# Modulation vectors, X's norm product and the first projection of a three-block transformer kernel: last quarters on TensorE, the product on ScalarE, three jobs begun by halves

## The reference, cut to what matters

```python
mod = c @ w_ada + b_ada            # c: 1024 values, w_ada: 1024 x 3072
shift, scale, gate = split(mod, 3)
xn = x * rsqrt(mean(x * x) + eps)
h = xn * g_norm * (1 + scale) + shift
proj = h @ w_in                    # 1024 x 5120, ten jobs of 512 columns
```

## Time and profile before

| | us |
|---|---|
| median of 3 runs (2044.94 to 2055.8) | 2050.69 |
| the profiled execution | 2051.03 |
| its span, first to last instruction | 2049.2 |
| TensorE busy | 1952.9 |
| VectorE busy | 1529.3 |
| ScalarE busy | 1262.1 |
| first matmul of the first projection starts | 30.62 |
| its second halves start | 51.22 |

### The profile page before, as it was taken

The page is one execution under the profiler, slowest core; times in us unless marked ns, Lnnn a source line. Parts: engine busy times, 40 slices in busy tenths (PEclk is TensorE's granted clock), DMA queues, the critical chain, the costliest instruction groups (busy, mean ns, idle before and its releaser), DMA issues. The chain is left out here.

```text
span 2049.2 us, 25968 instructions
## 1 busy us (share of the span) xinstructions
PE 1952.9 (95%) x9557; PEld 1611.3 (79%) x9557; DVE 1529.3 (75%) x1725; ACT 1262.1 (62%) x1366; POOL 95.1 (5%) x99
## 2 busy tenths in 40 slices
PE   4999998999999899999999999999999999999997
PEld 3887776788887788888888888888888878778876
DVE  7656766554577688889898888989988874467675
ACT  3544564534355477778777787877778764546453
POOL 0000300000000320000000000000000000000000
PEclk9999999999999999999999999999999999999999
DMA  9763644555552399999999999999999985524400
GB/s 354 250 226 131 206 154 164 176 187 185 164 185 83 117 391 371 380 381 368 385 364 379 377 378 377 364 394 365 371 387 365 386 298 180 190 79 154 144 1 31
DMA packets 186125, 535.14 MB, mean 261 GB/s; under 512 B 12465, under 2 KB 23749, under 8 KB 186054
## 3 DMA queue, kind: packets, MB, share of 16 engines
q1 hardware_dynamic: 179808, 518.95, 69.4%
q10 hardware_dynamic: 4422, 8.92, 1.2%
q0 software_dynamic: 1824, 6.31, 1.1%
HBM read 521.02 MB, written 13.12 MB: 261 GB/s over the span
## 5 line engine op out<-in xcount | busy, mean ns | idle before, releaser
L1107 DVE TENSOR_TENSOR WL<-ring,WH 128x2048 fp32r<-128x2048 f32 x475 | 1073.6, 2281 | 282.9 <-ACT WH L1103 279.6
L1103 ACT ACTIVATE WH<-ring 128x2048 fp32r<-128x2048 f32 x475 | 902.0, 1912 | 383.6 <-PE bank L457 352.2
L455 PE MATMUL bank<-WH,XTH 128*128 128x512 f32 (+3 forms) x1904 | 751.1, 394 | 19.1 <-DVE XTL L1852 6.5
L457 PE MATMUL bank<-WH,XTL 128*128 128x512 f32 (+3 forms) x1904 | 740.0, 389 | 0.0
L456 PE MATMUL bank<-WL,XTH 128*128 128x512 f32 (+3 forms) x1904 | 739.6, 388 | 0.0
L455 PEld LDWEIGHTS bank<-WH,XTH 128*128 128x128 f32 x1904 | 361.9, 190 | 105.3 <-DVE WL L1107 26.3
L457 PEld LDWEIGHTS bank<-WH,XTL 128*128 128x128 f32 x1904 | 361.7, 190 | 74.4
L456 PEld LDWEIGHTS bank<-WL,XTH 128*128 128x128 f32 x1904 | 362.2, 190 | 69.6 <-issue 0.2
L455 PE MATMUL bank<-WH,HTH 128*128 128x512 f32 (+1 forms) x568 | 219.9, 387 | 3.2 <-DVE HTL L2037 1.5
L457 PE MATMUL bank<-WH,HTL 128*128 128x512 f32 (+1 forms) x568 | 217.8, 383 | 0.0
L456 PE MATMUL bank<-WL,HTH 128*128 128x512 f32 (+1 forms) x568 | 217.7, 383 | 0.0
(11 more groups left out here) (420 smaller groups left out, 1358.2 us busy)
## 6 DMA issues: line engine op xcount, KB each, us to landing
ring<-in_od_we_gate SPq DMA_DIRECT2D x112, 1024.0 KB, 7.1
ring<-in_od_we_up SPq DMA_DIRECT2D x112, 1024.0 KB, 8.1
ring<-in_od_we_down SPq DMA_DIRECT2D x112, 1024.0 KB, 8.2
ring<-in_w_in SPq DMA_DIRECT2D x20, 1024.0 KB, 5.7
ring<-in_fox_w_in SPq DMA_DIRECT2D x16, 1024.0 KB, 6.3
ring<-in_nsa_w_in SPq DMA_DIRECT2D x14, 1024.0 KB, 5.1
ring<-in_w_ada SPq DMA_DIRECT2D x12, 1024.0 KB, 10.0
ring<-in_ev_w_in SPq DMA_DIRECT2D x12, 1024.0 KB, 5.2
```

Of the source, the lines that this page charges most:

```text
L455: nc.tensor.matmul(out, x[0], wt[0][:, k, :], start=start, stop=False, skip_group_check=check)
L457: return nc.tensor.matmul(out, x[1], wt[0][:, k, :], start=False, stop=stop, skip_group_check=check)
L1103: nc.scalar.activation(wh, slot_ap(n, nk, width), ACT.Copy).then_inc(hi_made, 1)
L1107: nc.vector.tensor_tensor(wl, slot_ap(n, nk, width), wh.bitcast(F32), ALU.subtract).then_inc(lo_made, 1)
```

## The change

```diff
+        def ada_part(kind, h, part):
+            n = chunk(kcols(w["w_ada"], {"scale": D, "shift": 0}[kind] + 512 * h, 512, 4 * part, 4), 4, 512)
+            ada[n] = kind, h, 4 * part, 4
+            if part and kind == "shift":
+                direct[n] = h
...
+            def out(self, c, tt):
+                return bank[4 + tt if c == 2 and self.by_parts == 3 else (2 * c + tt) % 4]
...
-                    if part == 0 and c >= 2:
+                    if part == 0 and c >= max(2, by_parts):
                         pe.wait_ge(proj_act, self.ba + c - 1)
...
+                        if (c, part, tt) in beside and k == 0:
+                            beside[c, part, tt]()
...
+                elif n in direct:
+                    eng.sem_inc(lo_made, 1)
                 elif n in ada:
...
                     reach(sp, lo_made, n - RING + 1, n)
+                if n - RING in direct:
+                    sp.wait_ge(ada_cols, 3 * direct[n - RING] + 2)
...
+            rms_act(act, XN)
+            scaled(act, "act_root")
+            for tt in range(TT):
+                nc.scalar.activation(XN[:, tt, :], X[:, tt, :], ACT.Copy, scale=stat[:, tt:tt + 1]).then_inc(xn_set, 1)
+            split_until(act, c_in1[0][0][0] + 1)
             act.dma_start(small[:, :], t["small"][0:NSM].partition_broadcast(128)).then_inc(small_in, 16)
             act.dma_start(co[:, :], t["co"]).then_inc(small_in, 16)
...
-            rms_act(act, XN)
-            split_until(act, c_in1[0][0][0] + 1)
...
             x_columns(1)
-            split_until(act, c_in1[0][1][0] + 1)
+            split_until(act, c_in1[2][0][0] + 1)
             act.wait_ge(ada_set, 4)
...
             rms(dve)
-            scaled(dve)
-            for tt in range(TT):
-                nc.vector.tensor_scalar(XN[:, tt, :], X[:, tt, :], stat[:, tt:tt + 1], None, ALU.mult).then_inc(xn_set, 1)
+            split_until(dve, 2)
...
             for h in range(2):
-                split_until(dve, c_in1[0][h][0])
-                out = bank[4 * h]
-                dve.wait_ge(ada_cols, 2 * h + 1)
+                if h:
+                    split_until(dve, c_in1[2][0][0] + 1)
+                dve.wait_ge(ada_cols, 3 * h + 1)
...
-                dve.wait_ge(ada_cols, 2 * h + 2)
-                nc.vector.tensor_tensor(SHIFT[:, 4 * h:4 * h + 4], bank[4 * h + 1][:, 0:4], vec_rows("b_ada", 4 * h, 4),
-                                        ALU.add).then_inc(ada_set, 1)
+                split_until(dve, c_in1[0][0][0] + 1 if h == 0 else c_in1[0][1][0])
+                dve.wait_ge(ada_cols, 3 * h + 3)
+                link(dve, nc.vector.tensor_tensor(shift_h, bank[4 * h + 1][:, 0:4], vec_rows("b_ada", 4 * h, 4), ALU.add))
+                nc.vector.tensor_tensor(shift_h, shift_h, bank[4 * h + 1][:, 4:8], ALU.add).then_inc(ada_set, 1)
                 dve.wait_ge(ada_set, 2 + 2 * h)
-                split_until(dve, c_in1[0][h][0] + 1)
...
+            def direct_columns(h, out):
+                n = [*direct][h]
+                pe.wait_ge(landed[n % RING], 16 * (n // RING + 1))
+                raw = slot_ap(n, 4, 512)
+                for m in range(4):
+                    for k in range(4):
+                        last = nc.tensor.matmul(out[:, 4 + m:5 + m], raw[:, k, 128 * m:128 * m + 128], C[:, 4 + k:5 + k],
+                                                start=k == 0, stop=k == 3, skip_group_check=True)
+                last.then_inc(ada_cols, 1)
...
             ada_columns("scale", 0, bank[0])
+            direct_columns(0, bank[1])
             ada_columns("shift", 0, bank[1])
             def other_columns():
                 T1.wait_tiles(pe, 4)
                 ada_columns("scale", 1, bank[4])
+                direct_columns(1, bank[5])
+                pe.wait_ge(ada_set, 3)
+
+            def last_columns():
                 ada_columns("shift", 1, bank[5])
+                pe.wait_ge(ada_set, 4)
             def heads1():
                 pe.wait_ge(roped1, 1)
-                pe.wait_ge(proj_act, P1.ba + 2)
+                pe.wait_ge(proj_act, P1.ba + 3)
...
-            P1.pe(pe, T1, {(0, 1): other_columns, 4: heads1, 6: differences, 8: mixed_groups}, by_parts=2)
+            P1.pe(pe, T1, {2: other_columns, (2, 0, 1): last_columns, 4: heads1, 6: differences, 8: mixed_groups})
```

More of the change, by code:

```diff
@@ L206, in build @@
         ada = {}
-        def ada_half(kind, h):
-            for n, k0, nk in cols(w["w_ada"], {"scale": D, "shift": 0}[kind] + 512 * h, 512):
-                ada[n] = kind, h, k0, nk
+        direct = {}
+        def ada_part(kind, h, part):
[3 more added lines that the diff above has]
+                direct[n] = h
         def in1_half(c, half_):
@@ L220, in build @@
         for h in range(2):
[L221 to L225, removed]
+            ada_part("scale", h, 0)
+            ada_part("scale", h, 1)
+            if h:
+                c_in1[2].append(in1_half(2, 0))
+            ada_part("shift", h, 0)
+            ada_part("shift", h, 1)
+            if h == 0:
+                c_in1[0].append(in1_half(0, 0))
+                c_in1[1].append(in1_half(1, 0))
+        for c in range(3):
+            c_in1[c].append(in1_half(c, 1))
+        for c in range(3, 10):
             c_in1[c] = cols(w["w_in"], in1_order[c], 512)
@@ L459, in build, with __init__, pe @@
         class Project:
-            def __init__(self, jobs, lhs, scale=None):
-                self.jobs, self.lhs, self.scale = jobs, lhs, scale
+            def __init__(self, jobs, lhs, scale=None, by_parts=0):
+                self.jobs, self.lhs, self.scale, self.by_parts = jobs, lhs, scale, by_parts
                 self.ba = base["proj_act"]
                 base["proj_act"] += len(jobs)
-            def pe(self, pe, operand, beside={}, late=None, by_parts=0):
+            def out(self, c, tt):
+                return bank[4 + tt if c == 2 and self.by_parts == 3 else (2 * c + tt) % 4]
+            def pe(self, pe, operand, beside={}, late=None):
+                by_parts = self.by_parts
                 steps = [(c, part) for part in range(2) for c in range(by_parts)]
@@ L490, in pe @@
                             operand.wait_tiles(pe, k0 + k + 1)
-                        last = three(bank[(2 * c + tt) % 4][:, 0:width], self.lhs(k0 + k, tt), wt, k,
+                        last = three(self.out(c, tt)[:, 0:width], self.lhs(k0 + k, tt), wt, k,
                                      k0 + k == 0, k0 + k == KD - 1, check=True)
@@ L501, in act @@
                     for tt in range(TT):
-                        last = nc.scalar.activation(dest(tt), bank[(2 * c + tt) % 4][:, 0:width], func,
+                        last = nc.scalar.activation(dest(tt), self.out(c, tt)[:, 0:width], func,
                                                     scale=stat[:, self.scale + tt:self.scale + tt + 1]
@@ L744, in build @@
         P1 = Project([(c_in1[i], 512, pcol(in1_order[i], 512), {512: ACT.Silu, 2560: ACT.Silu}.get(in1_order[i], ACT.Copy)
-                       if in1_order[i] < 3072 else ACT.Sigmoid) for i in range(10)], xt)
+                       if in1_order[i] < 3072 else ACT.Sigmoid) for i in range(10)], xt, by_parts=3)
         roped1 = sem("roped1")
@@ L1084, in accumulate @@
             acc = ADA_GATE if kind == "gate" else ADA_SUM[kind, h]
-            last_ = kind != "gate" and k0 + nk == KD
+            last_ = kind != "gate" and (kind == "shift" or k0 + nk == KD)
             for k in range(nk):
@@ L1832, in _ @@
             for h in range(2):
-                split_until(dve, c_in1[0][h][0])
-                out = bank[4 * h]
-                dve.wait_ge(ada_cols, 2 * h + 1)
-                scale_h = SCALE[:, 4 * h:4 * h + 4]
-                link(dve, nc.vector.scalar_tensor_tensor(out=scale_h, in0=out[:, 0:4], scalar=1.0,
+                if h:
+                    split_until(dve, c_in1[2][0][0] + 1)
+                dve.wait_ge(ada_cols, 3 * h + 1)
+                scale_h, shift_h = SCALE[:, 4 * h:4 * h + 4], SHIFT[:, 4 * h:4 * h + 4]
+                link(dve, nc.vector.scalar_tensor_tensor(out=scale_h, in0=bank[4 * h][:, 0:4], scalar=1.0,
                                                          in1=vec_rows("b_ada", 8 + 4 * h, 4), op0=ALU.add, op1=ALU.add))
                 nc.vector.tensor_tensor(scale_h, scale_h, vec_rows("g_norm", 4 * h, 4), ALU.mult).then_inc(ada_set, 1)
-                dve.wait_ge(ada_cols, 2 * h + 2)
-                nc.vector.tensor_tensor(SHIFT[:, 4 * h:4 * h + 4], bank[4 * h + 1][:, 0:4], vec_rows("b_ada", 4 * h, 4),
-                                        ALU.add).then_inc(ada_set, 1)
+                split_until(dve, c_in1[0][0][0] + 1 if h == 0 else c_in1[0][1][0])
+                dve.wait_ge(ada_cols, 3 * h + 3)
+                link(dve, nc.vector.tensor_tensor(shift_h, bank[4 * h + 1][:, 0:4], vec_rows("b_ada", 4 * h, 4), ALU.add))
```

(2 more changed lines are left out.)

## The result

The changed kernel took 2059.02 us (median of 20 runs, 2050.97 to 2071.62) against 2050.22 for the kernel before (20 runs beside it): 8.8 us slower, a ratio of 1.0041 with an interval of 1.0026 to 1.0057. The measured time lies 10.3 us above the predicted 2048.7 and 5.0 above the range's end of 2054. The profiled execution took 2062.25. Of the runs of before that are used further down, one took 3944.61 us; the ratios leave it out.

A forecast was written before the change was run, and what follows sets the result against it. TensorE, busy 1952.9 of 2049.2 us, was taken as the bound. Job 0 resuming 3.3 later with 5.3 us of matmuls already done wins 2.0, so the median 2050.69 becomes 2048.7; range 2043 to 2054.

The forecast's parts named there:

- Four columns cost 1.86 / 2 = 0.93: Before job 0, TensorE's four scale columns take half of the x8 row's 1.86 us, ending at 20.1.
- 16 products of 128x128 by one column, at the columns' 0.23, are 3.7 us: Before job 0, TensorE multiplies chunk 3 directly from 20.1 to 23.8, then does the shift columns to 24.8.
- VectorE's 25.75 hides this: VectorE finishes chunk 4's low part at 25.75, covering TensorE's direct products of chunk 3; uncovered they cost at most 3.7.
- 16 at 0.12 = 1.9: After the first halves of jobs 0 and 1, TensorE's direct product of chunk 10 takes 1.9 us, ending at 43.9.
- what follows the projection was to move with its end: Later stages hang on the first projection's end, which moves by as much as TensorE's resumption at 51.22.
- T: Time when h1's set of scale and shift is complete, forecast at 47.5 us against 48.18 before.
- the low stretch: Clock at 0.50, between 47.9 and 54.7 before, costing 1.7 us; the same loss was assumed behind TensorE's new wait.
- Rival (b): Low clock falls wholly under matmuls, 1.7 us more lost, perhaps another 0.9: 2051.3, slower than before; chance 16%.
- T + 7.0: Job 0 resumes at 54.5: after the set, columns 2.7, chunk 11's high part 1.9, low part 2.3, latency 0.1.
- The front: Up to job 0: X 1.1 earlier, its product 2.2 on ScalarE, transposes at 15.45, first matmul 28.85 against 30.62.
- Rival (c): At the start, X isn't early, its product takes 2.5, and the gain is waited for again: 2050.1; chance 14%.
- Rival (a): Chunk 11 is split during job 2, so job 0 resumes 4.4 earlier and the clock stays up: 2042.6; chance 6%.

The follow-up runs named there:

- the second profile: The changed kernel run again unedited, beside the kernel before on one chip: 2058.44 us, ratio 1.0039 (1.0021 to 1.0057).
- the added delay: Kernel before with 40 unused one-column products added between the two column groups of h1: 2066.53 us, ratio 1.0075 (1.0049 to 1.0101).

## Why the prediction was wrong

**The step that failed.** "Four columns cost 1.86 / 2 = 0.93", and from it "16 products of 128x128 by one column, at the columns' 0.23, are 3.7 us", "VectorE's 25.75 hides this", and in the second half "16 at 0.12 = 1.9". The rows' x8 was taken for eight products; it is four, with two records each. All prices of one-column products were half of the truth: 6.96 for the first sixteen, 5.75 (3.71 at the high clock) for the second. The cover of 25.75 was real (VectorE was done at 26.33), but the shift columns ended at 29.1 and not at 24.8, so it no longer hid them. A second step failed behind the first: what follows the projection was to move with its end and cost nothing of its own, and there the changed kernel lost 3.1 us more by the mask_past product. The estimate from the Trainium skill ("TensorE: Matmul & The Clock Gate", the section on LDWEIGHTS), 107 ns a weight load, is near one record at the high clock (0.116). By it the sixteen products would take an estimated 1.7 us; the measured times are 3.71 at the high clock and 6.96 at the low, and they decide.

**The sum to T** in the profile shown, against the forecast's 47.5:

| term | forecast | measured | difference |
|---|---|---|---|
| job 0 starts | 28.85 | 32.40 | 3.55 |
| first halves of jobs 0 and 1 | 12.66 | 13.51 | 0.85 |
| scale columns | 0.5 | 0.81 | 0.3 |
| direct products of chunk 10 | 1.9 | 5.61 | 3.7 |
| first tile of job 2 | 2.6 | 5.27 | 2.7 |
| shift columns, bias, wait | 1.0 | 1.72 | 0.7 |
| T | 47.5 | 59.3 | 11.8 |

The price of the products carries 2.8 of the first line (VectorE's wait), the third, about half of the fourth (3.71 - 1.9 = 1.8) and about half of the last: some 5.3 together. The clock carries about as much, an estimate of 5.8 in all. Its rise came at 37.6 and not at 34 (the second line), and then it fell: the mean was 0.80 from 46.7 to 49.0 and 0.50 from there, with TensorE busy for 3.30 of 3.30 us. That is 1.9 in the products and 2.7 in the tile, an estimate from 5.61 against 3.71 in the second profile and 5.27 against 2.6. I had put the low stretch under the hole behind T. Rival (b) had the right kind, low clock under work, and the right sign, but priced it at 2.6 in all. In the second profile T came at 52.46, 5.0 behind the forecast.

**Behind T the forecast held.** T + 7.0 was forecast and 7.1 measured (59.34 to 66.44), the hole 4.4 and 4.08, with WL as its end and no wait from there to the projection's end. Resuming 15.2 late with 5.3 us of matmuls done, 9.9 net, plus some 0.9 for twelve slow matmuls behind it (eight in before), gives the 10.8 at the attention.

**The front** was right too: X 1.1 earlier, product 2.19 (2.2 forecast), transposes at 15.39 (15.45). Rival (c) had two conditions that didn't come true, the late X and the product of 2.5. Its third did: what was won at the front was waited for again, at the shift columns (job 0 at 32.40, 30.62 before). Without the direct products and the new order the front keeps its 3.6 us. Rival (a), the hole closed, is what the two edits make; it couldn't come from the order as written.

**Why slower than before, then?** The mis-sized term explains about half of the miss at T, but not the loss against before, since the kernel without direct products is as slow. Shown: either of two edits of order, columns ahead of both tiles or the split of chunk 11 early, takes the ratio from 1.0041 (1.0026 to 1.0057) to 0.9992 or 0.9993 (neither above 1.0008), and both together to no better (1.0015; its upper end, 1.0035, overlaps the changed kernel's interval). At the mask_past product they stand at 284.98 and 289.10 in one profile each, the changed kernel at 296.03 on average of four. The chain is columns, set, six activations, high part, low part, resumption. The change puts a 5 us tile ahead of its last columns and chunk 11's split at its end, and then has only one tile to cover 7 us. Each edit alone lets the resumption follow directly on job 2.

**Still open.** The kernel without direct products reaches the attention at 163.5, 160.5 and 163.6 and the mask_past product at 291.3, 290.0 and 289.9, only 3.4 and 3.3 later than before on average, yet its 24 runs are 10 us slower. The rest arises in later stages: in their profiled executions 8.7 of 12.0 us come behind the mask_past product, and what the granted clock lacks from 300 us on is 10.7 more than in before (31.3 against 20.6 on average). What decides where such stretches fall was not settled. That they follow from when the stages start is argued only: the added delay hints at it, but its interval doesn't prove it.

## What to carry to other kernels

Before you price a product from a row, count its records against the code: here four products stood as x8, and halving the row's time halved every term built on it. When work moves to an engine whose queue already holds what the path waits for, price it as openly on the path unless the queue's next instruction is released later than the new work ends. Of two covers for one gap (tiles behind the set, or an early split) one is enough; before you build a new order, look whether it leaves neither. And where a gain of 3 to 5 us is to be shown, add up the low clock of the later stages before you believe or drop it.

## What the runs showed of the hardware that wasn't expected

- A float32 product of 128 x 128 with one column is two records: 32 in 3.71 us at the high clock (0.116 each) and in 6.96 at the low (0.22; low by the pace of the records there). Forty such products are 80. Float32 transposes are one record each (16 in 3.67).
- The granted clock fell to 0.50 while TensorE was busy without a pause on one-column products (46.7 to 52.3 us).
- The clock in the first 60 us differs between executions of one program: attention at 161.37 to 169.20. Later stretches at the low clock, up to 20.5 us, hide a gain of 3 to 5 us at the front.
- In the first 37 us the column of the granted clock can stand at 1.00 while the matmuls run at half the pace (starts 0.43 us apart up to 37.6, 0.23 behind).
